# Row gathers of two expert pairs at once, from split rows, and a smaller ring of expert places

## The reference, cut to what matters

```
group_prob = softmax(xt @ wg_r + bg_r);  gp, gi = top_k(group_prob, 1)          # 4 groups
top_logits, ei = top_k(in_group, 2);     weights = gp * softmax(top_logits)      # 2 of 4 experts
combine = sum(one_hot(expert_id, 16) * weights)                                  # 256 x 16
h = silu(einsum('td,edf->etf', xt, w_gate)) * einsum('td,edf->etf', xt, w_up)    # 16 x 256 x 512
h = h * combine.T[:, :, None]
return einsum('etf,efd->td', h, w_down)
x = layer_norm(DEEPNORM_ALPHA * x + ffn, ln2_g, ln2_b)
```

## Time and profile before

| | |
|---|---|
| median of three executions | 1325.45 us |
| the profiled execution's own time | 1324.61 us |
| its span (first to last instruction) | 1322.9 us |
| TensorE (PE) busy | 1308.2 us, 99% |
| VectorE (DVE) busy | 569.2 us, 43% |
| ScalarE (ACT) busy | 476.6 us, 36% |
| read from HBM | 361.96 MB, 275 GB/s over the span |
| experts, first gather to last scatter | 859.8 to 1308.7 us |

### The profile page before, as it was taken

How to read it: one execution, slowest core, us unless ns; L and a number is a source line. 1 busy time by engine, 2 the same in 40 slices (tenths; PEclk the granted TensorE clock), 3 DMA queues, 4 the chain that set the end, 5 groups by cost and what they waited for, 6 DMA issues and landing times.

```text
span 1322.9 us, 17951 instructions
## 1 busy us (share of the span) xinstructions
PE 1308.2 (99%) x7379; PEld 959.7 (73%) x7379; DVE 569.2 (43%) x741; ACT 476.6 (36%) x667; POOL 29.5 (2%) x55
## 2 busy tenths in 40 slices
PE   9999999999999999999999999999999999999998
PEld 9999989998888888888888888844453444544443
DVE  4367445356555644464455555525112121221206
ACT  4535343346556544454333433422121121211212
POOL 1000000400000000000100001000000000000000
PEclk9999999999999999999999999999999999999999
DMA  9965555544454445554556795699999999999996
GB/s 302 344 230 197 175 190 188 190 160 160 159 161 156 160 154 194 174 174 159 191 190 226 262 393 178 264 416 416 422 420 422 420 421 421 421 421 420 422 408 253
DMA packets 122100, 364.97 MB, mean 276 GB/s; under 512 B 11627, under 2 KB 19243, under 8 KB 98486
## 3 DMA queue, kind: packets, MB, share of 16 engines
q1 hardware_dynamic: 115430, 359.06, 73.1%
q10 hardware_dynamic: 6608, 5.02, 1.3%
HBM read 361.96 MB, written 2.10 MB: 275 GB/s over the span
## 4 chain that ended last, share of the span: by engine, by line
PE 93%; DMA 3%; DVE 2%; ACT 0%; issue 0%; SPq 0%; DVEq 0%; ACTq 0%
PE main L1212 19%; PE main L1214 19%; PE main L1213 19%; PE main L556 16%; PE att L646 7%; PE att L510 5%; DMA mraw<-in_expert_w_down_dram 3%; PE att L1453 1%; PE main L522 1%; PE main L523 1%; PE att L1436 1%; PE att L1472 1%; PE att L1468 1%; DVE wlo L1866 1%; PE att L1423 0%; PE att L617 0%
## 5 line engine op out<-in xcount | busy, mean ns | idle before, releaser
L1866 DVE TENSOR_TENSOR wlo<-raw,whi 128x2048 fp32r<-128x2048 f32 x135 | 310.3, 2299 | 360.3 <-ACT whi L1619 360.3
L1619 ACT ACTIVATE whi<-raw 128x2048 fp32r<-128x2048 f32 x135 | 258.1, 1912 | 420.4 <-PE main L1214 418.9
L556 PE MATMUL main<-mraw,xg 128*64 128x512 f32 x1024 | 225.4, 595 | 1.5 <-DMA mraw<-in_expert_w_up_dram 1.4
L1212 PE MATMUL main<-whi,xhi 128*128 128x512 f32 (+1 forms) x544 | 203.9, 375 | 0.0
L1214 PE MATMUL main<-whi,xlo 128*128 128x512 f32 (+1 forms) x544 | 201.7, 371 | 0.0
L1213 PE MATMUL main<-wlo,xhi 128*128 128x512 f32 (+1 forms) x544 | 201.6, 371 | 0.0
L556 PEld LDWEIGHTS main<-mraw,xg 128*64 128x64 f32 x1024 | 72.1, 137 | 137.4 <-issue 136.2
L1212 PE MATMUL main<-xhi,whi 128*128 128x256 f32 (+1 forms) x560 | 159.6, 285 | 1.1 <-DVE wlo L1997 1.0
L1213 PE MATMUL main<-xlo,whi 128*128 128x256 f32 (+1 forms) x560 | 158.4, 283 | 0.0
L1214 PE MATMUL main<-xhi,wlo 128*128 128x256 f32 (+1 forms) x560 | 158.4, 283 | 0.0
L1214 PEld LDWEIGHTS main<-whi,xlo 128*128 128x128 f32 x544 | 102.5, 188 | 17.7
(11 more groups left out here) (336 smaller groups left out, 1300.8 us busy)
## 6 DMA issues: line engine op xcount, KB each, us to landing
raw<-in_w_in_dram SPq DMA_DIRECT2D x95, 1024.0 KB, 5.1
mraw<-in_expert_w_gate_dram SPq DMA_DIRECT2D x64, 1024.0 KB, 21.3
mraw<-in_expert_w_up_dram SPq DMA_DIRECT2D x64, 1024.0 KB, 22.4
mraw<-in_expert_w_down_dram SPq DMA_DIRECT2D x58, 1024.0 KB, 23.1
raw<-in_w_branch_dram SPq DMA_DIRECT2D x24, 1024.0 KB, 5.0
raw<-in_w_out_dram SPq DMA_DIRECT2D x16, 1024.0 KB, 7.9
mraw<-in_expert_w_down_dram SPq DMA_DIRECT2D x12, 512.0 KB, 9.3
xin<-in_x_dram SPq DMA_DIRECT2D x4, 512.0 KB, 8.2
```

What stands on the lines that cost most here:

```text
L556: ins = pe.matmul(main[0][half, w, :], xg[:, k, half], src[:, kk * DE:(kk + 1) * DE], start=(k == 0), stop=(k == KT - 1))
L1212: pe.matmul(o, ah, bh, start=start, stop=False, skip_group_check=skip)
L1619: act.activation(whi[:, u % SPLIT, 0:n], raw[:, slot, 0:n], ACT.Copy).then_inc(hi_done, 1)
L1866: dve.tensor_tensor(wlo[:, u % SPLIT, 0:n], raw[:, slot, 0:n], whi[:, u % SPLIT, 0:n].bitcast(F32), ALU.subtract).then_inc(lo_done, 1)
```

## The change

Four things.

1. In pairs 2 and 4 (`DOUBLE`) the gather serves the pair and the one after it: `hot` holds four experts (256 columns), `gather_two(q)` makes fp32r products with 256 moving columns, from two parts of the rows, `xrh` and `xrl`, and ScalarE fills two `xg`. Pairs 3 and 5 have no gather of their own; they begin with gate_up(0), and put(0), put(1) come behind it. ScalarE writes `xrh` (two copies) and VectorE `xrl` (two subtractions) during pair 1. `xrl` overwrites `xr`, so pairs 6 and 7 have to gather from the parts too: there `gather(q, split=True)` makes two fp32r products of 128 moving columns where one float32 product was.
2. `xrh` and the second `xg` take three places out of the ring, from unit 43 (`SHRUNK`) on: MRAW goes from 19 to 16.
3. The loads of units 14 and 16 wait for U1 + 14 used units instead of U1 + 16, and unit 15 is loaded in halves for U1 + 15 and U1 + 16. SyncE issues 14 and 16 ahead of 11.
4. `xg` and the pair `yhi`, `ylo` change sides in the same memory, so that place 16 is the half that is free first.

```diff
-MRAW = 19
+MRAW = 16
+DOUBLE = (2, 4)
-        ring = second_round[:4] + [NP, NP + 1] + second_round[4:]
+        grown = second_round[:4] + [NP, NP + 1] + second_round[4:]
+        SHRUNK = GROWN + 6
+        kept_for_x = grown[6:9]
+        ring = grown[9:] + grown[:6]
         def place(g):
             if g < NP:
                 return g
-            return second_round[g - NP] if g < GROWN else ring[(g - GROWN) % MRAW]
+            if g < GROWN:
+                return second_round[g - NP]
+            return grown[g - GROWN] if g < SHRUNK else ring[(g - SHRUNK) % MRAW]
+        xrh, xrl = at("xrh", places[kept_for_x[0]], [P, T, D], F32R), at("xrl", made["xlo"], [P, T, D], F32R)
+        xgs = xg, at("xg_second", places[kept_for_x[2]], [P, KT, 2 * SLOTS])
@@ first_units, moe_loads
+                elif r in (once[0], once[2]):
+                    sp.wait_ge(unit_used, U1 + 3 * QUADS + 2)
+                elif r == once[1]:
+                    for i in range(2):
+                        sp.wait_ge(unit_used, U1 + 3 * QUADS + 3 + i)
+                        load_half(sp, r, i)
-            first_units(sp, range(6, NP))
+            first_units(sp, (*range(6, 11), once[0], once[2], *range(11, once[0]), once[1], *range(once[2] + 1, NP)))
@@ TensorE
-            def gather(q):
+            def gather(q, split):
                 for k in range(4 * q, 4 * q + 4):
+                    o = att[:, q, k % 4 * P:(k % 4 + 1) * P]
                     for t in range(T):
-                        ins = pe.matmul(att[:, q, k % 4 * P:(k % 4 + 1) * P], xr[:, t, k * P:(k + 1) * P], hot[:, t, :],
+                        rows, cols = hot[:, t, 0:2 * SLOTS], slice(k * P, (k + 1) * P)
+                        if split:
+                            pe.matmul(o, xrh[:, t, cols], rows, ...)
+                            ins = pe.matmul(o, xrl[:, t, cols], rows, ...)
+                        else:
+                            ins = pe.matmul(o, xr[:, t, cols], rows.bitcast(F32), ...)
+            def gather_two(q, m):
+                if q >= 2:
+                    pe.wait_ge(xg_out, m * 4 + 2 * (q - 1))
+                for kk in range(4):
+                    o, cols = att[:, q % 2 * 2 + kk // 2, kk % 2 * 256:(kk % 2 + 1) * 256], ...
+                    for t in range(T):
+                        pe.matmul(o, xrh[:, t, cols], hot[:, t, :], ...)
+                        ins = pe.matmul(o, xrl[:, t, cols], hot[:, t, :], ...)
+                if second:
+                    gate_up(0)
+                    put(0)
+                    put(1)
+                    gate_up(1)
+                    put(2)
+                elif fixed in DOUBLE:
+                    pe.wait_ge(x_lo, 8 + T)
+                    put(0)
+                    put(1)
+                    gather_two(0, m)
+                    put(2)
                     pe.wait_ge(y_lo, m * 4)
+                    gather_two(1, m)
+                    gate_up(0)
+                    gather_two(2, m)
+                    gate_up(1)
+                    gather_two(3, m)
+                else:
+                    split = fixed is None
+                    ...
@@ ScalarE, end of the copies of pair 1
+                if static and m + 1 == DOUBLE[0]:
+                    for t in range(T):
+                        act.activation(xrh[:, t, :], xr[:, t, :], ACT.Copy).then_inc(x_hi, 1)
@@ VectorE, pair 1
+                if static and m + 1 == DOUBLE[0]:
+                    for t in range(T):
+                        dve.wait_ge(x_hi, 8 + t + 1)
+                        dve.tensor_tensor(xrl[:, t, :], xr[:, t, :], xrh[:, t, :].bitcast(F32), ALU.subtract).then_inc(x_lo, 1)
```

More of the change, by code:

```diff
@@ L228, in build @@
         xT = at("xT", made["sig"], [P, 4, S])
-        xg = at("xg", made["qaT"], [P, KT, 2 * SLOTS])
-        yhi, ylo = at("yhi", made["qbT"], [P, 2, 512], F32R), at("ylo", made["qbT"] + 4096, [P, 2, 512], F32R)
+        xg = at("xg", made["qbT"], [P, KT, 2 * SLOTS])
+        yhi, ylo = at("yhi", made["qaT"], [P, 2, 512], F32R), at("ylo", made["qaT"] + 4096, [P, 2, 512], F32R)
         places = [O1, O1 + 8192, made["xhi"], made["xhi"] + 8192, made["acc"], made["acc"] + 8192]
@@ L234, in build @@
         once = range(len(places), len(places) + 3)
-        places += [O2, O2 + 8192, made["qbT"]]
+        places += [O2, O2 + 8192, made["qaT"]]
         assert made["sig"] + 8192 <= made["cT"] + 2048
@@ L244, in build @@
         GROWN = NP + len(second_round)
-        ring = second_round[:4] + [NP, NP + 1] + second_round[4:]
-        assert len(ring) == MRAW
+        grown = second_round[:4] + [NP, NP + 1] + second_round[4:]
+        SHRUNK = GROWN + 6
+        kept_for_x = grown[6:9]
+        ring = grown[9:] + grown[:6]
+        assert len(ring) == MRAW and places[kept_for_x[1]] == places[kept_for_x[0]] + 8192
         def place(g):
@@ L268, in build @@
         dg = at("dg", made["ksT"], [P, T, P])
[L269 removed]
+        hot = carve(0, "hot", [P, T, 4 * SLOTS], F32R)
+        lgT = at("lgT", small[0], [P, S])
+        cmb = carve(0, "cmb", [P, T, 2 * SLOTS])
         bw = at("bw", made["ksT"], [P, KT, NG + NE])
[L271 removed]
+        wsl = carve(0, "wsl", [P, S], F32R)
         assert small[0] <= made["ksT"] + 8192
@@ L372, in loads_of @@
         def loads_of(g):
-            return 2 if NP <= g < NP + 4 else 1
+            return 2 if NP <= g < NP + 4 or g == once[1] else 1
         centre_order = (0, 5, 1, 2, 3, 6, 4, 7)
@@ L538, in step @@
                 fixed = m if turns is None else None
+                second = fixed is not None and fixed - 1 in DOUBLE
+                xg = xgs[1] if second else xgs[0]
                 def unit(r):
@@ L567, in step @@
                 pe.wait_ge(hot_ok, 1 + m)
[L568 to L576, removed]
-                    pe.wait_ge(y_lo, m * 4)
-                gather(3)
+                if second:
+                    gate_up(0)
[9 more added lines that the diff above has]
+                    put(2)
+                    pe.wait_ge(y_lo, m * 4)
+                    gather_two(1, m)
[3 more added lines that the diff above has]
+                    gather_two(3, m)
+                else:
+                    split = fixed is None
+                    put(0)
+                    gather(0, split)
+                    put(1)
+                    gather(1, split)
+                    put(2)
+                    gate_up(0)
+                    gather(2, split)
+                    gate_up(1)
+                    if fixed != 0:
+                        pe.wait_ge(y_lo, m * 4)
+                    gather(3, split)
                 pe.wait_ge(cmb_ok, 1 + m)
                 pe.wait_ge(sc_free, 1 if fixed == 0 else m * 8 - 1)
+                rows = slice(2 * SLOTS, 4 * SLOTS) if second else slice(0, 2 * SLOTS)
                 for t in range(T):
-                    pe.transpose(main[1][:, 1, t * P:(t + 1) * P], hot[:, t, :], ident[:])
+                    pe.transpose(main[1][:, 1, t * P:(t + 1) * P], hot[:, t, rows].bitcast(F32), ident[:])
                 for t in range(T):
@@ L680, in act_tail, with pair_step @@
             act.activation(ed[:], ed[:], ACT.Exp).then_inc(ed_out, 1)
-            def pair_step(m, final, first=False):
+            def pair_step(m, final, static=False):
+                first = static and m == 0
                 for q in range(4):
[L684 to L688, removed]
+                    if static and m in DOUBLE:
+                        act.wait_ge(xg_ps, 2 * q + 2 + m * 4)
+                        for n, rows in enumerate(xgs):
+                            for kk in range(4):
+                                k = 4 * q + kk
+                                c0 = kk % 2 * 256 + n * 2 * SLOTS
+                                ins = act.activation(rows[:, k, :], att[:, q % 2 * 2 + kk // 2, c0:c0 + 2 * SLOTS], ACT.Identity,
+                                                     bias=gbT[:, KT + k:KT + k + 1], scale=gbT[:, k:k + 1])
+                            ins.then_inc(xg_out, 1)
+                    elif not (static and m - 1 in DOUBLE):
+                        act.wait_ge(xg_ps, 1 + q + m * 4)
+                        for k in range(4 * q, 4 * q + 4):
+                            ins = act.activation(xg[:, k, :], att[:, q, k % 4 * P:(k % 4 + 1) * P], ACT.Identity,
+                                                 bias=gbT[:, KT + k:KT + k + 1], scale=gbT[:, k:k + 1])
+                        ins.then_inc(xg_out, 1)
                     if first and q == 1:
                         act.activation(warm[:, 2:3], rowok[:], ACT.Silu)
+                if static and m + 1 == DOUBLE[0]:
+                    for t in range(T):
+                        act.activation(xrh[:, t, :], xr[:, t, :], ACT.Copy).then_inc(x_hi, 1)
                 act.wait_ge(ws_t, 1 + m)
@@ L781, in dve_moe, with slots @@
             link(dve.tensor_copy(pos[:].rearrange("p t e -> p (t e)"), r_[:, 0:T * NE]))
-            def slots(pair, n):
```

(15 more changed lines are left out.)

21 lines of the change are left out of this document (15 added, 6 removed).

## The result

The changed kernel took 1328.41 us (median of ten executions, 1328.07 to 1330.36) against 1325.57 us for the kernel before (ten, 1324.6 to 1326.46): a ratio of 1.0025, 95% interval 1.0016 to 1.0033. It is slower, by 2.8 us. I had forecast slower, but by 8.5 us, three times as much. The loss comes from the place that my smaller term had named, the loads of units 43 and 44; the larger term, 14.3 us for the gathers of pairs 6 and 7, is not there at all.

The account below looks back on a forecast made before the run. The end was taken as the later of the loads' line and TensorE's line. 0.4 + 14.3 - 5.9 = +8.8 us on 1324.61 us gave 1333.4, by the median 1334.2, forecast 1334 us; range 1326.5 to 1338.

Parts of the forecast that it names:

- my smaller term: Loads of units 43 and 44 under the ring of 16: the queue runs dry, loads' line 2.3 us later.
- What bounds the kernel: Expert stage: TensorE sets the pace mid-stage, loads are 4.8 us a pair slower; the end is the later line.
- Part 1, the gathers of pairs 2 to 5: Double gathers: TensorE gains 9 to 10 us by the end of pair 5, none reaching the end by itself.
- Part 2, the gathers of pairs 6 and 7: Split gathers at 0.224 us a product, the upper bound: 7.2 us more a pair, +14.3 us for two.
- Part 3, the early loads: Loads of units 14 to 16: first 20 units up to 5.0 us early, 3.1 us left at unit 20.
- Part 4, the ring of 16: Unit 44 waits for unit 28, issued at 931.1, lands at 935.9 us: DMA line 2.3 us behind.
- The sum: Whole kernel: 0.4 us later into pair 6, +14.3 us of gathers, -5.9 us of vanished waits: +8.8 us.
- rival A: 128-column fp32r products are cheap, 0.085 to 0.17 us; the loads' line sets the end: +2.3 us, 1327.7 us; chance 0.20.
- the dear products: The forecast case: 128-column fp32r products in pairs 6 and 7 cost 0.224 us each; 1334 us; chance 0.60.
- B: Queue doesn't run dry at unit 44, products are cheap, the early loads' 5.0 us reach the end: 1320.4 us; chance 0.07.
- D: TensorE, not the loads, sets the end, so the gathers' gain reaches it: +4.8 us, 1330 us; chance 0.06.
- C: Products are dear and the queue runs dry more often, as at unit 48: 1338 us and above; chance 0.07.

Follow-up runs that it names:

- r3: The changed kernel with every pair gathering for itself in float32 and no parts made; ring of 16 and early loads kept: 1328.53 us, ratio 1.0025.
- r4: The changed kernel with the products of the gathers of pairs 6 and 7 in full float32 instead of fp32r: 1336.12 us, ratio 1.0081.
- r2: The kernel before with only the early loads and the side swap, ring of 19, gathers as before: 1325.4 us, ratio 1.0001.
- r6: The changed kernel with 64 instead of 128 stationary columns in each fp32r product of pairs 6 and 7: 1328.41 us.
- r8: The kernel before with the early loads, and units 24 to 27 and 34 to 36 loaded in halves: 1325.34 us, ratio 0.9999.

## Why the prediction was wrong, point by point

- **What bounds the kernel.** Right. In the middle TensorE sets the pace while the loads fall behind, and the end is the later of two lines. r3 and r4 show both sides: 9.9 us of TensorE's time weigh nothing while it is the earlier line, and 14 us more of it make it the later.
- **Part 1, the gathers of pairs 2 to 5.** Right. The 64 products of a double gather come 0.12 us apart; the stalls behind VectorE's adds (of the puts, and of the transposes of `hot`, L643) were 3.6 us, where I had 5. After two of the four pairs TensorE was 4.2 us ahead (put(0) of pair 4 at 1072.56 instead of 1076.79 us), which makes 8.5 us for four; I had 9 to 10, a little much. All of it turned into waits.
- **Part 2, the gathers of pairs 6 and 7.** This is the step that failed. "I take the upper end", 0.224 us for a product of 128 columns; measured, 0.11 us. +14.3 us became about 0 (pair 6: 0.35 us more work). The measured price lies between my bounds, but I chose by the likeness of the line and not by what the rows of all forms have in common. The row that answers it was there: a float32 product is two instructions 0.112 us apart, and an fp32r product of 256 columns takes 0.12. The two move 128 and 256 columns and yet have nearly the same spacing, and what they share is a weight load of 128 x 128. That already speaks for the weight load. And the earlier trace rows, which I read as 0.085 us for a product, was an average over unlike ones: the four products start 0.03, 0.11 and 0.11 us apart in the trace, so the lower bound was too low. The Trainium skill (TensorE: Matmul & The Clock Gate, LDWEIGHTS) says that a weight load takes about its number of columns divided by 1.2, in ns; by it, as an estimate, 107 ns for 128 columns and 53 for 64. The traces agree, with 0.11 and 0.06 us. The sustained 81 ns for 128 moving columns, which the Trainium skill gives on the same page (Back-to-back issue gap) and which I weighed instead, doesn't hold for these products: they came 0.11 us apart.
- **Part 3, the early loads.** Right in kind: the lead is lost on the way. It was 3.3 us at unit 19 and not 5.0, since the nine units behind unit 10 took 23.9 us and not 22.4 at the full rate; it was 2.7 us at unit 20 (3.1 foretold), and gone at unit 26.
- **Part 4, the ring of 16.** The issue and the landing of unit 44 are right to 0.1 us. But I took the lag of the whole line, 2.3 us, from this landing, and compared a load alone in an empty queue with one in a full queue. Counted in what the DMA engines moved, the hole was 3.4 us, and 0.4 us came behind it. This is the second term that was mis-sized. I had seen the weak point at unit 48 (0.5 us of cover): issued 2.6 us before unit 47 landed, it took 6.2 us and not 4.7, but the engines were hardly idle then, at 406 GB/s from 938 to 950 us.
- **The sum.** With the two numbers put right the sum ends on the loads' line: 3.4 + 0.4 = +3.8 us on the profiled execution, where the last wait for a load ends 3.6 us later (median +2.8). This is rival A, at 1327.7 us in the prediction, with a deeper hole. I gave it 0.20 and the dear products 0.60. The wrong confidence lies there: for a form that no row showed, with bounds 9 us apart, I had put three times the weight on one end. That the time did go up, as I had said, is owed to the ring's term and not to the one that made most of my sum.
- **Rivals.** B (faster) falls with the hole at unit 44, and r2 shows that its 5.0 us were not to be had with the full ring either. D falls with r3. C's mechanism (the queue runs dry more often) has at most the 0.4 us behind 938 us.

## What to carry to other kernels

When two resources are both full, ask first which line the end hangs on. Work taken off the other one, here 9 us, shows up only as waiting, and here a lower clock for a moment came behind the longest of these waits. What buffers cost that are given up can hang on the moment and not on their number, as with the three places here: look at how far ahead of the landing before it each load was issued, and try the place where that distance is long. Size a hole in a queue by the bytes that were not moved, not by how late one load landed. And before pricing an instruction in a form that no row shows, compare the spacing of all forms that share an operand; what they have in common is likely the limit.

## What the runs showed of the hardware

- At a granted clock of 1.00 and with 128 stationary columns, fp32r products follow each other at 0.11 us for 64 and 128 moving columns and at 0.12 us for 256; a float32 product of 128 is two instructions 0.112 us apart. With 64 stationary and 128 moving columns it is 0.06 us (r6). A split gather of 128 columns thus costs as much as the float32 one, and here only the wider moving side makes fp32r pay.
- A load issued to an idle queue landed after 4.7 us (unit 44). When a load landed out of a full queue, 0.45 MB of the loads behind it had moved as well, so the two landings differ by 1.1 us for the same hole.
- Behind 2.2 and 2.3 us without work TensorE's granted clock was 0.50 for 3.4 us (the changed kernel from 1180.26, r4 from 1185.73 us).
- The DMA engines can be busy all the time and move 256 GB/s in place of 412 (r8, 872 to 876 us); why, no run shows.
